# Spreading rows of decay sums in the state-space blocks: accumulating transfers onto a mask in SBUF in place of group-table products

## The reference: what is computed

```
dA = (dt * A)                      # per token and head
a_cs = cumsum(dA) in the chunk
Lmat[l, s] = exp(a_cs[l] - a_cs[s]) where s <= l, else 0
cb = C . B^T                       # per chunk and group
y_diag = (cb * Lmat) . (x * dt)
```

## Time and profile before

| | |
|---|---|
| Median of 3 runs | 2277.94 us (2277.85 to 2278.59) |
| The profiled execution | 2278.16 us, its span 2276.3 us |
| Granted TensorE clock | 0.998 of full speed |
| Busy: TensorE, VectorE, ScalarE, GpSimd | 99%, 71%, 56%, 19% |

### The profile page before, as it was taken

The page is one execution under the profiler, slowest core; times in us unless marked ns, Lnnn a source line. Parts: engine busy times, 40 slices in busy tenths (PEclk is TensorE's granted clock), DMA queues, the critical chain, the costliest instruction groups (busy, mean ns, idle before and its releaser), DMA issues.

```text
span 2276.3 us, 33664 instructions
## 1 busy us (share of the span) xinstructions
PE 2254.4 (99%) x12336; PEld 2102.1 (92%) x12336; DVE 1612.4 (71%) x2671; ACT 1275.3 (56%) x2616; POOL 441.5 (19%) x512
## 2 busy tenths in 40 slices
PE   8999999999999999999999999999999999999998
PEld 7999779899899999999989996898989999999997
DVE  7988785365588867766679778735655888678566
ACT  5555445555466666666446545455555666666662
POOL 1211002310112232231111210022001122332320
PEclk9999999999999999999999999999999999999999
DMA  5555326852375696788655453278324665976984
GB/s 161 115 113 110 94 84 149 182 133 66 60 181 145 148 194 131 173 186 230 124 122 109 101 119 95 65 180 180 104 55 86 173 172 128 196 148 152 197 234 108
DMA packets 128705, 313.10 MB, mean 138 GB/s; under 512 B 14678, under 2 KB 28246, under 8 KB 128548
## 3 DMA queue, kind: packets, MB, share of 16 engines
q0 software_dynamic: 72128, 135.30, 34.7%
q1 hardware_dynamic: 55844, 175.19, 24.5%
q10 hardware_dynamic: 576, 0.52, 0.1%
HBM read 276.36 MB, written 34.60 MB: 137 GB/s over the span
## 4 chain that ended last, share of the span: by engine, by line
PE 91%; DVE 4%; DMA 2%; ACT 1%; issue 1%; SPq 0%; POOL 0%; DVEq 0%; ACTq 0%
PE G L1342 28%; PE M L1861 8%; PE G L1861 8%; PE M L1872 6%; PE G L1872 6%; PE G L1909 2%; PE M L1877 2%; PE G L1877 2%; PE M L1866 2%; PE G L1866 2%; PE M L1305 2%; PE M L1307 2%; PE M L1306 2%; PE M L1342 1%; DVE tap L2084 1%; PE M L1571 1%
## 5 line engine op out<-in xcount | busy, mean ns | idle before, releaser
L636 POOL DMA_DIRECT2D wlo<-wstream x236 | 208.9, 886 | 1061.8 <-ACT wlo L687 889.8
L687 ACT ACTIVATE wlo<-raw 128x512 fp32r<-128x512 f32 x220 | 138.1, 628 | 304.7 <-PE G L1342 228.5
L1342 PE MATMUL G<-A_hi,whi 128*128 128x384 f32 x864 | 293.4, 340 | 9.9 <-DVE A_lo L2044 9.5
L1342 PE MATMUL G<-A_hi,wlo 128*128 128x384 f32 x864 | 289.6, 335 | 0.0
L649 POOL DMA_DIRECT2D w_low<-wstream x192 | 166.0, 868 | 615.6 <-ACT w_low L1059 615.6
L1342 PE MATMUL G<-A_lo,whi 128*128 128x384 f32 x864 | 284.7, 335 | 0.0
L1070 ACT ACTIVATE whi<-raw 128x384 fp32r<-128x384 f32 (+1 forms) x224 | 128.9, 575 | 117.7 <-DVE raw L2613 73.4
L1070 ACT ACTIVATE whi<-raw_b 128x384 fp32r<-128x384 f32 (+1 forms) x224 | 128.9, 575 | 110.4 <-DVE raw_b L2613 71.8
L1342 PEld LDWEIGHTS G<-A_hi,whi 128*128 128x128 f32 x864 | 162.9, 189 | 13.9 <-issue 11.8
L1342 PEld LDWEIGHTS G<-A_lo,whi 128*128 128x128 f32 x864 | 162.4, 188 | 1.0
L1342 PEld LDWEIGHTS G<-A_hi,wlo 128*128 128x128 f32 x864 | 162.6, 188 | 0.0
(11 more groups left out here) (555 smaller groups left out, 6161.2 us busy)
## 6 DMA issues: line engine op xcount, KB each, us to landing
raw<-wstream SPq DMA_DIRECT2D x172, 512.0 KB, 4.7
wlo<-wstream POOLq DMA_DIRECT2D x236, 256.0 KB, 5.3
w_low<-wstream POOLq DMA_DIRECT2D x96, 256.0 KB, 4.8
w_low<-wstream POOLq DMA_DIRECT2D x96, 192.0 KB, 3.9
down_sum<-staged POOLq DMA_DIRECT2D x48, 384.0 KB, 7.8
raw_b<-wstream SPq DMA_DIRECT2D x32, 512.0 KB, 7.5
raw_b<-wstream SPq DMA_DIRECT2D x32, 384.0 KB, 4.1
raw<-wstream SPq DMA_DIRECT2D x32, 384.0 KB, 4.2
```

The source lines that it names most:

```text
L636: pool.dma_start(low, wstream[stream(L, c)][:, part], accum_op=ALU.add).then_inc(lo_in[c % 2][h], 16)
L687: act.activation(wlo[:, s, part], raw[:, s, part], ACT.Copy, scale=-1.0).then_inc(neg_done, 1)
L1342: last = mm(out, w, p[:, k, a:b], start=(k == 0 and w is w_hi and p is parts[0]), stop=(k == KT - 1 and (w is w_lo and only is None or onl ...
```

## The change

The table products go. The sums, 48 rows of 128 for each direction, are transposed within tile 8 (hook at k = 5), copied to `cum_rows` and stored to a DRAM tensor `cum_kept` by two DMAs from ScalarE's queue. The masks are laid by ScalarE into `expd` in SBUF instead of into the banks (`lay_mask`), for block 0 too; GpSimd issues for each block two accumulating DMAs, one for each direction, that read 4 rows (2 KB) of `cum_kept` into each of the 128 partitions and add them onto the mask (`spread`). The Exp then works in place in `expd`. `expd` has two sets, so the mask of block n + 1 needs `weights(n - 1)` done. VectorE's tables, `cum2`, `cumT` and `wide` go.

```
+            def spread(L, n):
+                t, g = n // 2, n % 2
+                if n == 0:
+                    pool.wait_ge(cum_out, 32 * (L + 1))
+                for d in range(2):
+                    pool.wait_ge(mask_in, L * 24 + 2 * n + d + 1)
+                    rows = cum_kept[L, d, t * HEADS + 4 * g:t * HEADS + 4 * g + 4, :]
+                    pool.dma_start(expd[2 * (n % 2) + d][:, :, :].rearrange("p h l -> p (h l)"),
+                                   rows.rearrange("(o h) l -> o (h l)", o=1).to_broadcast([P, 4 * P]),
+                                   accum_op=ALU.add).then_inc(cum_s, 16)
...
                 for c in range(0 if L else AHEAD, C_MLP):
                     low_halves(L, c)
+                    if 9 <= c < 9 + TT * GROUPS:
+                        spread(L, c - 9)
...
+                def lay_mask(n):
+                    for d in range(2):
+                        act.activation(expd[2 * (n % 2) + d][:, :, :],
+                                       c_("maskf", 0, 2 * P).rearrange("p (d l) -> p d l", d=2)[:, d:d + 1, :].to_broadcast([P, 4, P]),
+                                       ACT.Copy).then_inc(mask_in, 1)
                     if j == 8:
                         act.wait_ge(cum_t, L + 1)
-                        act.activation(cumT[:, :, :], MB[2][:, 128:384].rearrange("p (d l) -> p d l", d=2),
-                                       ACT.Copy).then_inc(cum_hi, 1)
+                        act.activation(cum_rows[0:48, :, :], MB[2][0:48, 128:384].rearrange("p (d l) -> p d l", d=2),
+                                       ACT.Copy).then_inc(cum_r, 1)
+                        act.wait_ge(cum_r, L + 1)
+                        for d in range(2):
+                            act.dma_start(cum_kept[L, d], cum_rows[0:48, d, :]).then_inc(cum_out, 16)
+                        lay_mask(0)
...
+                        act.wait_ge(cum_s, 32 * (L * 12 + n + 1))
                         for d in range(2):
                             for h in range(4):
-                                ins = act.activation(expd[2 * (n % 2) + d][:, h, :], MB[2 + d][:, h * P:(h + 1) * P], ACT.Exp,
-                                                     bias=ncum[:, d, t, 4 * g + h:4 * g + h + 1])
+                                e = expd[2 * (n % 2) + d][:, h, :]
+                                ins = act.activation(e, e, ACT.Exp, bias=ncum[:, d, t, 4 * g + h:4 * g + h + 1])
                         if n < 11:
-                            act.wait_ge(ssd_e, L * 24 + 2 * n + 2)
-                            for d in range(2):
-                                act.activation(MB[2 + d].rearrange("p (h l) -> p h l", h=4),
...
+                            if n:
+                                act.wait_ge(ssd_w, L * 12 + n)
+                            lay_mask(n + 1)
...
             if n:
                 pe.wait_ge(cb_c, L * 12 + n)
-                pe.wait_ge(ssd_e, L * 24 + 2 * n)
             else:
-                pe.wait_ge(wide_r, L * 2 + 2)
-                pe.wait_ge(tab_r, L * 3 + 3)
...
-            pe.matmul(MB[0][:, 0:P], bcf[:, g, tk], bcf[:, 2 + g, tk], start=True, stop=True)
-            for d in range(2):
-                out = MB[2 + d].rearrange("p (h l) -> p h l", h=4)
-                if n:
-                    pe.wait_ge(mask_in, L * 22 + 2 * (n - 1) + d + 1)
-                    last = pe.matmul(out, group_r[:, n:n + 1].to_broadcast([P, P]), wide[:, d, :, :], start=False, stop=True,
...
+            pe.matmul(MB[0][:, 0:P], bcf[:, g, tk], bcf[:, 2 + g, tk], start=True, stop=True).then_inc(ssd_mm, 1)
...
-                        last = turn(MB[2][:, (d + 1) * P:(d + 2) * P], cum2[:, d, :], ident)
+                        last = turn(MB[2][0:48, (d + 1) * P:(d + 2) * P], cum[:, d, :, :].rearrange("p c h -> p (c h)"), ident)
...
-                    project(8 + n, None, (lambda: diag(pe, L, n - 2)) if n >= 2 else (lambda: blocks(pe, L, 0)) if n else None)
-                    if n == 0:
-                        turn_cum()
-                    else:
+                    project(8 + n, None, (lambda: diag(pe, L, n - 2)) if n >= 2 else (lambda: blocks(pe, L, 0)) if n else turn_cum,
+                            (5,) if n == 0 else None)
+                    if n:
                         blocks(pe, L, n)
...
-                dve.tensor_copy(ident_r[:, :], ident).then_inc(tab_r, 1)
...
-                link(dve.memset(cum2[:, :, :], 0.0))
...
-                for d in range(2):
-                    for part in range(2):
-                        link(dve.tensor_copy(cum2[:, d, part * 64:part * 64 + 48], MB[2][:, d * 48:(d + 1) * 48]))
...
-                dve.wait_ge(cum_hi, L + 1)
-                link(tt(cumT[64:128, :, :], MB[2][64:128, 128:384].rearrange("p (d l) -> p d l", d=2), f_(cumT[64:128, :, :]),
-                        ALU.subtract))
-                for d in range(2):
-                    tt(wide[:, d, :, :], f_(cumT[:, d:d + 1, :]).to_broadcast([P, 4, P]),
```

More of the change, by code:

```diff
@@ L100 @@
 CONST["g_first"] = CONST["alt"] + 1
-CONST["group"] = CONST["g_first"] + 8
-CONST["head"] = CONST["group"] + 12
-CONST["stack"] = CONST["head"] + 4
+CONST["stack"] = CONST["g_first"] + 8
 CONST["eps"] = CONST["stack"] + 16
@@ L161, with build_trunk @@
 SCRATCH = 4096
-def build_trunk(nc, xT, memT, wstream, dft, fw3, params, consts, x_kept, down_sum, yT):
+def build_trunk(nc, xT, memT, wstream, dft, fw3, params, consts, cum_kept, x_kept, down_sum, yT):
     ctx = ExitStack()
@@ L227, in build_trunk @@
         wxh, wxl = place("wxh", [P, D], oRING, F32R), place("wxl", [P, D], oRING + 4096, F32R)
[L228 to L233, removed]
+        cum_rows = place("cum_rows", [P, 2, P], oRING)
         ncum = place("ncum", [P, 2, TT, HEADS], oRING + 7744)
@@ L416, in build_trunk @@
         mask_in = sem("mask_laid")
-        tab_r, cum_t, cum_hi, wide_r = sem("rounded_tables"), sem("cum_turned"), sem("cum_hi"), sem("cum_spread")
+        cum_t, cum_r, cum_out, cum_s = sem("cum_turned"), sem("cum_rows_copied"), sem("cum_rows_out"), sem("cum_spread")
         ssd_mm, cb_c, ssd_e, ssd_w, ssd_y = (sem(n) for n in (
@@ L1255, in blocks @@
                 pe.wait_ge(cb_c, L * 12 + n)
-                pe.wait_ge(ssd_e, L * 24 + 2 * n)
             else:
-                pe.wait_ge(wide_r, L * 2 + 2)
-                pe.wait_ge(tab_r, L * 3 + 3)
                 pe.wait_ge(x_c, L * 9 + 6)
                 pe.wait_ge(silu_d, L * 16 + 16)
-            pe.matmul(MB[0][:, 0:P], bcf[:, g, tk], bcf[:, 2 + g, tk], start=True, stop=True)
-            for d in range(2):
-                out = MB[2 + d].rearrange("p (h l) -> p h l", h=4)
-                if n:
-                    pe.wait_ge(mask_in, L * 22 + 2 * (n - 1) + d + 1)
-                    last = pe.matmul(out, group_r[:, n:n + 1].to_broadcast([P, P]), wide[:, d, :, :], start=False, stop=True,
-                                     skip_group_check=True)
-                    continue
-                pe.matmul(out, group_r[:, n:n + 1].to_broadcast([P, P]), wide[:, d, :, :], start=True, stop=False)
-                last = pe.matmul(out, ident_r[:, :], mask_r[:, d:d + 1, :].to_broadcast([P, 4, P]), start=False, stop=True)
-            last.then_inc(ssd_mm, 1)
+            pe.matmul(MB[0][:, 0:P], bcf[:, g, tk], bcf[:, 2 + g, tk], start=True, stop=True).then_inc(ssd_mm, 1)
         def diag(pe, L, n):
@@ L2171, in _ @@
                 flat = lambda a: a[:, :, :, :].rearrange("p d c h -> p (d c h)")
-                dve.tensor_copy(ident_r[:, :], ident).then_inc(tab_r, 1)
-                dve.tensor_copy(mask_r[:, :, :].rearrange("p d l -> p (d l)"), c_("maskf", 0, 2 * P)).then_inc(tab_r, 1)
-                dve.tensor_copy(group_r[:, :], c_("group", 0, 12)).then_inc(tab_r, 1)
-                link(dve.memset(cum2[:, :, :], 0.0))
                 project(6)
@@ L2897, in constants @@
     out[:, CONST["g_first"]:CONST["g_first"] + KT] = i["norm_mix"][0].reshape(KT, P).T
-    row = np.arange(P) % 64
-    used = row < 48
-    out[used, CONST["group"] + row[used] // 4] = 1
-    out[used, CONST["head"] + row[used] % 4] = 1
     rows = np.arange(P)
@@ L3047 @@
     args = [nc.dram_tensor(n, a.shape, F32, kind="ExternalInput").ap() for n, a in arrays.items()]
+    cum_kept = nc.dram_tensor("cum_kept", (DEPTH, 2, TT * HEADS, P), F32, kind="Internal").ap()
     x_kept = nc.dram_tensor("x_kept", (KT, P, T), F32, kind="Internal").ap()
@@ L3050 @@
     yT = nc.dram_tensor("yT", (D, T), F32, kind="ExternalOutput").ap()
-    build_trunk(nc, *args, x_kept, down_sum, yT)
+    build_trunk(nc, *args, cum_kept, x_kept, down_sum, yT)
     r = run_bass_kernel_spmd(nc, [arrays], core_ids=[0])
```

3 lines of the change are left out of this document (removed).

## The result

| | median | runs | ratio to before, 95% |
|---|---|---|---|
| before | 2277.89 us | 4 (2277.04 to 2278.59) | |
| changed | 2305.82 us | 4 (2301.66 to 2312.36) | 1.0125 [1.0113, 1.0137] |

The change costs 28 us where 11 were forecast. The profiled execution is the quickest of the four: 2301.66 us, its span 2299.7, so 23.4 us more than that of before in span. The other three are up to 10.7 us longer; before scatters by 1.5.

A forecast was written before the change was run, and what follows sets the result against it. TensorE, busy 99% of the span, was taken to bound the kernel. Product savings of 6.1 us a layer against waits from the new loop gave +5.6 a layer, +11.2 in all: 2289 us, range 2267 to 2314.

The forecast's parts named there:

- The step freed by the products: TensorE, block to block: without the table products 0.47 us less a block, step 9.45 us in place of 9.92.
- The wait of the transposes: TensorE in mid tile 8: stands still about 1.15 us a layer until VectorE's sums are ready.
- The Exp released by a DMA in every block: ScalarE's Exp: it would wait for the spread's transfers, no longer for TensorE.
- hidden transfers: Rival: second spread lands within 5.1 us, loop at most 9.05, a layer -4.3 us; 2269 us; chance 0.28.
- lateness kept: Rival: landing 5.1 to 5.5 us, no step held, but block 11's lateness eats the 5.2 saved; 2278 us; chance 0.17.
- the slower read: Rival: all partitions reading the same 2 KB lands at 7.5 us, loop 11.5, +23 us a layer; 2325 us; chance 0.17.
- The plain turn: Loop from one Exp group's end to the next: mask, issue, landing, Exp and handovers, 9.87 us (8.2 to 10.9).
- the section on the new loop: Exp waits for two transfers, masks follow the Exp before: 0.56 + 1.04 + 5.9 + 2.17 + 0.2 = 9.87 us.
- the sum a layer: 1.15 - 0.93 - 5.2 + 1.4 + 3.8 + 5.4 = +5.6 us a layer, two layers +11.2.
- tile 10 and the nine steps behind it: TensorE waits 0.7 us at tile 10, 0.7 at tile 11, then nine steps at 9.87 instead of 9.45: 3.8.
- 5.4 at the end: Gate section: TensorE waits 5.4 us for block 11's weights before `diag(11)`.
- the forecast's own: The case that the loop paces, landing 5.5 to 6.9 us: range 2283 to 2308 us; chance 0.38.

The follow-up runs named there:

- e1: The kernel before without the products with the group table in blocks 1 to 11; 2267.54 us against 2277.27, ratio 0.9954.
- e3: The changed kernel with each spread reading 128 different rows of 2 KB in place of one row for all partitions; 2310.79 us, ratio 1.0140.
- e2: The changed kernel without the spread of block 0, whose Exp waits only for its mask; 2300.27 us, ratio 1.0096.
- e5: The changed kernel with the transposes of the sums at k = 6 of tile 8, one place later; 2306.57 us, ratio 1.0125.
- e10: The changed kernel with tile 10's chunk split before the first mask and its low halves issued before the first spread; 2313.62 us, ratio 1.0152.
- e12: The changed kernel with the raw load for tile 11 held until the first spread has landed; 2305.75 us, ratio 1.0119.
- e4: The changed kernel with three buffer sets of `expd` and masks laid two blocks ahead; 2278.69 us, ratio 1.0006.
- e13: e11 with the second mask laid only after the first Exp and spreads in the changed kernel's order; 2273.42 us, ratio 0.9982.
- e14: The kernel before, with tile 12's first product waiting for an added 64 KB store in each layer; 2284.38 us against 2277.15, ratio 1.0032.
- e11: e4 with the raw load for tile 11 held until the first spread has landed; 2275.22 us, ratio 0.9990.
- e9: e4 with tile 10's low halves before the first spread, first mask behind that chunk's split, block 1's mask behind cb's copy; 2283.82 us, ratio 1.0025.
- e6: e4 with the raw load of tile 10 held until the first spread has landed; 2290.55 us, ratio 1.0050.

## Why the prediction was wrong in size

The direction, the place and the mechanism were right, and the sum was too small: +11.2 forecast, 28 measured. The profiled pair differs by 23.4, and this I can account for.

**Right.** The step freed by the products (9.45 forecast, 9.47 measured; the whole saving 9.7 us in e1). The wait of the transposes (1.15, 1.02). The Exp released by a DMA in every block. Refuted among the rivals: hidden transfers and lateness kept, which needed a landing of the second spread of at most 5.1 and 5.5 us, where none of the 24 landed in less than 5.94; and the slower read (e3).

**Right by luck.** The plain turn (9.87 forecast, 10.03 measured). Two of its terms were off and nearly cancel. The second issue follows 0.54 us behind the first, not 1.04: the 1.04 of the earlier trace rows is the distance of the two `wlo` halves on ScalarE, not GpSimd's own pace. And the landing is 6.2 from there, not 5.9. ScalarE's timeline of the kernel before:

```profile
101.75 0.62 ACT L687 ACTIVATE wlo<-raw 128x512 fp32r<-128x512 f32 x1
...
102.80 0.62 ACT L687 ACTIVATE wlo<-raw 128x512 fp32r<-128x512 f32 x1
```

**The step that failed.** It is the section on the new loop, in two terms: the landing, taken as 5.9 us, and the Exp, taken as 2.17. In the sum a layer, tile 10 and the nine steps behind it stood for 0.7 + 0.7 + 3.8 = 5.2 us. They cost 4.25 (13.72 - 9.47) and 9.7 (94.96 - 9 x 9.47). With them, and 4.0 in place of 5.4 at the end, the sum comes to 12.8, where the first layer's end came 14.2 us later than before (the first product with `rmem_bc` at 274.82, before at 260.63). The 1.4 left I did not trace.

The Exp shows why, since it paces TensorE here. I had the first Exp done at 112.5 and each of eleven more 9.87 later: the last at 221.1. It was done at 229.5 (227.03 + 2.44), 8.4 us later, and this is nearly all of the layer's excess of 8.6 over the forecast's 5.6:
- *The landing of the first spread.* Taken as 5.9 from the second issue; it was 8.4 (103.94 to 112.38): 2.3 us in the Exp's end. The Trainium skill ("DMA: Bandwidth & Descriptors", the anatomy of a GpSimd DMA) would have it at an estimated 2.6; no spread here landed in less than 3.9. I had cited the pair that landed at 6.9 beside one raw load, and then had two spreads, two low halves and a raw load in the same 9 us.
- *The turn.* 10.42 in place of 9.87, 11 times: 6.1 us. The mean landing of these eleven was 6.6 us, and the Exp took 2.45 us in SBUF, where it took 2.17 from the bank: 0.28 a turn. About as much a turn comes from one landing alone, that of 8.94. I had put one number for a quantity that here ran from 5.9 to 8.9.

In the second layer the end came another 11.5 us later (1412.71, before 1387.03), 5.9 above the forecast: the first Exp was about 1.7 late, and the turn of 10.24 makes 4.1. Behind that point, where the code is the same, the profiled execution of the changed kernel was 2.3 us shorter. From one execution to the next the total moved by 10 us. That the landings do this too is argued, not shown: one execution of the kernel was profiled. But the mean turn of a layer runs from 10.17 to 10.97 us over the profiles of the changed kernel and of e2, e3, e5, e10 and e12 (to 10.78 without e3, which reads other rows). With 22 turns, 0.5 us a turn is the size of that scatter.

**Where the waits lie is not what they cost.** For tile 10 I forecast 0.7 us and it was 4.25: a wait of 2.46, and then the granted clock. The changed kernel, by microsecond:

```profile
114.00:115.00 1.00, 1.00 (x5) 1.00 (x6) 0.04 (x1) 1.00 (x4) 0.00 (x0) 0.84 0.23 41
115.00:116.00 1.00, 1.00 (x4) 1.00 (x4) 0.97 (x2) 1.00 (x3) 0.34 (x1) 0.50 0.00 0
116.00:117.00 1.00, 1.00 (x4) 1.00 (x4) 0.97 (x2) 1.00 (x3) 1.00 (x3) 0.50 0.00 0
117.00:118.00 1.00, 1.00 (x5) 1.00 (x5) 0.93 (x3) 1.00 (x3) 1.00 (x3) 0.50 0.73 123
```

I first took this 4.25 as a term of its own. The end of the layer says no: the product with `rmem_bc` starts 45.3 us behind the end of the last Exp in the changed kernel (229.48 to 274.82), in e2 (223.88 to 269.16) and in e3 (235.62 to 280.91), whatever tile 10 waited: 2.46, nothing and 1.72. While the loop paces the blocks, such a loss on TensorE is paid out of waits that it would have had later. Only a clock that falls behind the last Exp adds to it: 48.3 in e12, where it stood at 0.50 for 10 us from 229.3. In e4, where nothing else paces, the loss at tile 10 counts: e4 to e13 is 5.3 us for the start's transfers moved apart. What e13 still has over e1 is 6 us. Of it about 5 are found: waits for low halves among the blocks (2.12, and 1.11 in the second layer), 1.8 for the clock behind the first, 2.0 for the sums, less 1.9 for block 0's products, which e1 keeps. The end of the layer was forecast as one wait of 5.4; it came as three (1.02, 1.69 and 1.24), 4.0 in all.

**Which choice was wrong.** The range held the time (2305.8 in 2267 to 2314), and so did the forecast's own, 2283 to 2308. The number lay near the cheap end of it, with one landing for all turns, chosen between 4.2 (worked out from a DMA alone) and 6.9 (a pair beside one raw load).

**Left open.** Whether some order of transfers removes the last wait at tile 11 too. And why a turn's landing is 6 us once and 9 another time: the rows show a raw load and low halves beside it, and e12 that one such load is worth 2 us at the start; no run isolates it in the later turns.

## What to carry to other kernels

When an edit turns a product into a transfer, look for the buffer that ties the transfer to the step before: two sets made a loop of 10 us around a step of 9.5, and a third set took 27 of 28 us back with the same bytes. Price a transfer by its landing at the load that the edit creates, as a range, and multiply the upper part of that range by the number of turns. And name as a cost what bounds the end of the chain, not the largest wait: a wait that is removed ahead of a loop changes nothing (e5).

## What the runs showed of the hardware

- After a stand-still of 2.2 us TensorE's granted clock is at the 1.2 GHz level for 3.4 us, and the stand-still costs about 4.0 us (e14). The same stands behind waits of 2.46 and 2.01 us in the changed kernel and of 2.12 in e13 (123.17). Behind waits of 1.24 us (169.48), of 2.29 in e11 (122.89), and even of 2.60 and 3.30 in e3 (126.54, 1369.45) the clock stayed at 1.00: from 2 to 3.3 us it goes either way. Around longer ones the low level could last longer: 6.8 us around one of 4.56 (e9), 10.2 around one of 5.32 (e6), but 3.4 behind one of 4.48 (e10).
- Eight Exp of 128 x 128 in place in SBUF took 2.45 us, out of a PSUM bank 2.17.
- An adding DMA of 256 KB onto SBUF landed after 3.9 us at the least, 5.4 in the median and 8.9 at the most (48 spreads). The first of a pair landed after 3.9 to 4.8 us, the second, issued 0.54 us behind it, after 5.9 to 8.9. A raw load of 512 KB beside them was worth 2 us. The changed kernel's answer on the tile `expd`:

```profile
DMA to landing us min/median/max: 3.9/5.4/8.9
```
- Reading one 2 KB row into 128 partitions was no slower than reading 128 rows of 2 KB: 2305.8 against 2310.8 us, mean turns of 10.42 and 10.24 against 10.97 and 10.73 (e3).
